# The recurrent mixer of a two-layer kernel: chunks inverted in pairs half a period apart, with the serial part one chunk behind

## The reference, cut to what matters

```python
def rwkv7_step(state, inp):
    r_t, w_t, k_t, v_t, kk_t, a_t = inp
    sa = jnp.einsum('bhvk,bhk->bhv', state, -kk_t)
    state = (state * w_t[:, :, None, :] + sa[..., None] * (kk_t * a_t)[:, :, None, :]
             + v_t[..., None] * k_t[:, :, None, :])
    y = jnp.einsum('bhvk,bhk->bhv', state, r_t)
    return state, y
...
    _, y = lax.scan(rwkv7_step, s0, (tm(rh), tm(wh), tm(kh), tm(vh), tm(kk), tm(ah)))
    mean = jnp.mean(y, axis=-1, keepdims=True)
    var = jnp.mean(jnp.square(y - mean), axis=-1, keepdims=True)
    y = (y - mean) * lax.rsqrt(var + GN_EPS)
...
    mix = jnp.concatenate([o_nsa, o_rwkv], axis=-1).astype(x.dtype)
    return x + mix @ w_out
```

## Time and profile before

| what | us |
|---|---|
| median of 3 runs | 2627.87 |
| lowest and highest of them | 2627.56 and 2632.1 |
| the profiled execution's own time | 2630.19 |
| its span, first to last instruction | 2628.2 |
| PE busy | 2567.8 |
| DVE busy | 1561.6 |
| ACT busy | 1108.6 |
| POOL busy | 425.6 |

### The profile page before, as it was taken

How to read it: one execution, slowest core, us unless ns; L and a number is a source line. 1 busy time by engine, 2 the same in 40 slices (tenths; PEclk the granted TensorE clock), 3 DMA queues, 4 the chain that set the end, 5 groups by cost and what they waited for, 6 DMA issues and landing times.

```text
span 2628.2 us, 46698 instructions
## 1 busy us (share of the span) xinstructions
PE 2567.8 (98%) x19224; PEld 2086.1 (79%) x19224; DVE 1561.6 (59%) x2521; ACT 1108.6 (42%) x2067; POOL 425.6 (16%) x381
## 2 busy tenths in 40 slices
PE   8999999999999999999999999999999999999998
PEld 6887777778778998899888777766776677788876
DVE  8765443436686665676546676355567646656754
ACT  3242233323355543556335554324445545344521
POOL 4421221100000000000000000111112100456644
PEclk9999999999999999999999999999999999999999
DMA  6753443134423454534534222631011253100032
GB/s 227 212 119 107 97 131 101 65 115 165 160 102 116 144 192 141 189 132 150 170 127 173 76 96 90 270 129 49 29 49 49 85 189 105 42 19 19 19 129 96
DMA packets 80754, 307.24 MB, mean 117 GB/s; under 512 B 7200, under 2 KB 8864, under 8 KB 62624
## 3 DMA queue, kind: packets, MB, share of 16 engines
q1 hardware_dynamic: 55984, 238.72, 25.9%
q0 software_dynamic: 12800, 33.56, 5.6%
q10 hardware_dynamic: 11760, 31.99, 3.2%
HBM read 268.32 MB, written 69.47 MB: 129 GB/s over the span
## 4 chain that ended last, share of the span: by engine, by line
PE 83%; DVE 9%; ACT 4%; issue 3%; DMA 1%; POOL 1%; DVEq 0%; ACTq 0%; SPq 0%; POOLq 0%
PE ps L425 46%; PE ps L3270 4%; PE ps L1258 4%; PE ps L1257 4%; PE ps L1259 4%; PE ps L2145 2%; PE ps L2191 2%; PE ps L2171 2%; PE ps L2072 2%; PE ps L609 2%; PE ps L635 1%; PE ps L2074 1%; PE ps L2073 1%; PE ps L624 1%; DVE parts L404 1%
## 5 line engine op out<-in xcount | busy, mean ns | idle before, releaser
L425 PE MATMUL ps<-parts,parts 128*128 128x512 f32 (+2 forms) x6456 | 1467.5, 387 | 15.9 <-DVE parts L804 8.8
L425 PEld LDWEIGHTS ps<-parts,parts 128*128 128x128 f32 x6456 | 1171.6, 188 | 299.7 <-issue 34.3
L404 DVE TENSOR_TENSOR parts<-ring,parts 128x1024 fp32r<-128x1024 f32 x180 | 220.8, 1238 | 174.7 <-ACT parts L381 166.3
L381 ACT CAST parts<-ring 128x1024 fp32r<-128x1024 f32 x183 | 188.7, 1044 | 116.9 <-DMA ring<-in_weights 62.1
L1257 PE MATMUL ps<-parts,parts 128*128 128x256 f32 x840 | 236.2, 281 | 1.3 <-ACT phase_data L1406 1.3
L1258 PE MATMUL ps<-parts,parts 128*128 128x256 f32 x840 | 236.1, 281 | 0.0
L1259 PE MATMUL ps<-parts,parts 128*128 128x256 f32 x840 | 236.0, 281 | 0.0
L404 POOL TENSOR_TENSOR parts<-ring,parts 128x1024 fp32r<-128x1024 f32 x62 | 153.2, 2472 | 423.1 <-DVE parts L381 423.0
L2552 POOL TENSOR_TENSOR phase_data<-phase_data,stream 128x512 f32<-128x512 f32 x12 | 17.2, 1436 | 1186.2 <-PE ps L2082 1186.2
L867 DVE TENSOR_TENSOR_SCAN stream<-stream 128x513 f32<-128x513 f32 (+3 forms) x96 | 95.2, 992 | 173.2 <-ACT stream L737 173.0
L1257 PEld LDWEIGHTS ps<-parts,parts 128*128 128x128 f32 x840 | 158.7, 189 | 2.4 <-ACT phase_data L1406 1.5
(11 more groups left out here) (391 smaller groups left out, 3761.6 us busy)
## 6 DMA issues: line engine op xcount, KB each, us to landing
ring<-in_weights SPq DMA_DIRECT2D x128, 1024.0 KB, 4.9
up_sums<-in_weights POOLq DMA_DIRECT2D x24, 1024.0 KB, 8.9
ring<-in_weights SPq DMA_DIRECT2D x32, 512.0 KB, 4.3
ring<-up_sums SPq DMA_DIRECT2D x30, 512.0 KB, 5.9
phase_data<-up_sums SPq DMA_DIRECT2D x60, 256.0 KB, 5.6
up_sums<-up_sums POOLq DMA_DIRECT2D x8, 1024.0 KB, 5.4
phase_data<-in_weights SPq DMA_DIRECT2D x30, 256.0 KB, 5.5
raw_keep<-phase_scratch SPq DMA_DIRECT2D x21, 256.0 KB, 2.4
```

The source lines that it names most:

```text
L381: cast(self.hi(p), self.whole(p)).then_inc(self.k.hi_ready, 1)
L404: g.tensor_tensor(self.lo(p), self.whole(p), self.hi(p).bitcast(F32), ALU.subtract).then_inc(self.k.lo_ready, 1)
L425: last = pe.matmul(out, a, b, start=i == 0 and a is ah and b is bh, stop=i == len(pairs) - 1 and a is al)
```

## The change: what it does

Every product of the inversion covers all four head pairs at once, so that there is one wait, one ACT copy and one DVE addition per product where there were two. The two banks of `inv_x` and the two of `inv_w` now belong to even and odd chunks. Iteration c (there are 18) holds levels 0 to 2 of chunk c, levels 3 to 5 of chunk d = c-1, and the serial part of chunk e = c-2. Level 5 multiplies only the 32x32 blocks that are not zero, from `mab` without a mask, so that POOL makes five masked copies and not six.

`raw`, `masked` and `both_heads` of chunk c+1 stay in iteration c, and the operands are made two chunks ahead on POOL, the exponentials three chunks ahead on ACT. There are more buffers for this: five for `ra`, three for `bk`, four for `mm`, three for `mab`. Two of the `ra` and one of the `mm` buffers lie in the ring slot of the third weight unit of the projection, which is therefore loaded only after the last `y_part`; another `mm` buffer lies in a place for a weight's high part.

The normalisation of the first four tiles stands in iterations 10 to 14 where it stood in 8 to 13. Half of projection tile 0 stands in iteration 16, the rest of it and two of eight parts of tile 1 in iteration 17.

The buffers and the loads:

```diff
@@ -2673,7 +2675,7 @@
         load_weights(k, sp, START["in3", 1] + 5)
         sp.wait_ge(gated, 8)
         sp.dma_start(io["mix_keep"], k.data(12544, 4096)).then_inc(k.spilled.sem, 16)
-        load_weights(k, sp, START["wout", 0] + RING)
+        load_weights(k, sp, START["wout", 0] + RING - 1)
         sp.wait_ge(raw_in, 48)
 
...
-    b.ra = [x.rearrange("p (c d) -> p c d", c=4) for x in (view_cp(k, 2560), low(0, 4 * P), low(512, 4 * P))]
+    lent = RING_AT + (START["wout", 0] + 2) % RING * SLOT
+    b.ra = [x.rearrange("p (c d) -> p c d", c=4) for x in (
+        view_cp(k, 2560), low(0, 4 * P), low(512, 4 * P), k.view(lent, 4 * P), k.view(lent + 512, 4 * P))]
...
-    mm, mab = low(3072, 4, 4 * P).rearrange("p (a b) (c d) -> p a b c d", a=2, c=4), four_of(low(5120, 2, 4 * CHUNK))
+    mab = four_of(low(5120, 2, 4 * CHUNK))
+    spare = HI_AT + (k.later_pieces.base + len(k.later_pieces.what) + 3) % 4 * (SLOT // 2)
+    mms = [four_of(x) for x in (low(3072, 2, 4 * P), low(4096, 2, 4 * P), k.view(lent + 1024, 2, 4 * P),
+                                k.data(spare, 2, 4 * P))]
+    mabs = (mab[:, 0], mab[:, 1], early(0, CHUNK))
...
-    x_bank, w_bank, G = (2, 4), (3, 7), (slice(0, 2), slice(2, 4))
+    XS, WS, TS, GS = LEVELS, LEVELS - 1, LEVELS - 1, LEVELS
+    x_bank, w_bank = (2, 4), (3, 7)
...
+    pieces.not_before[pieces.base + 4] = 2
...
         sp.wait_ge(y_mm, C)
+        load_weights(k, sp, START["wout", 0] + RING)
         sp.dma_start(gate[1], part("gate_keep", 1)).then_inc(gate_in[1], 16)
         x_again(1)
         load_weights(k, sp, START["wout", 0] + 4)
```

The body of `inv_x` and `inv_w`:

```diff
+            else:
+                pe.wait_ge(t_ready[i], TS * n + l)
+                if l < LEVELS - 1:
+                    pe.wait_ge(off_ready, MASKS * c + l + 1)
+                    last = product(c, x_out(c, l), off[:, i, l], tt[:, i])
                 else:
-                    pe.wait_ge(t_ready[i], (LEVELS - 1) * c + l)
-                    last = group_pairs(i, x_bank[i], 0, lambda m, e: off[rows(e), c % 2, l, m],
-                                       lambda m, e: tt[rows(e), 0, m])
-                last.then_inc(x_mm[i], 1)
+                    for m in range(4):
+                        for e in range(2):
+                            upper, lower = slice(64 * e, 64 * e + 32), slice(64 * e + 32, 64 * e + 64)
+                            last = pe.matmul(x_out(c, l)[lower, m, 0:32], mab(c)[upper, m, 32:64],
+                                             tt[upper, i, m, 0:32], start=True, stop=True)
+            last.then_inc(x_mm[i], 1)
...
+            i, n = c % 2, c // 2
+            pe.wait_ge(x_ready[i], TS * n + l)
+            pe.wait_ge(g_ready[i], GS * n + l)
+            if l < LEVELS - 1:
+                product(c, t_out(c), gg(c), xx[:, i])
+                last = product(c, w_out(c, l), xx[:, i], gg(c))
+            else:
+                for m in range(4):
+                    for e in range(2):
+                        upper, lower = slice(64 * e, 64 * e + 32), slice(64 * e + 32, 64 * e + 64)
+                        last = pe.matmul(w_out(c, l)[upper, m, 32:64], xx[lower, i, m, 0:32],
+                                         gg(c)[lower, m, 32:64], start=True, stop=True)
+            last.then_inc(w_mm[i], 1)
```

The order of PE:

```diff
-        for c in range(C + 1):
-            if c >= 1:
-                state_part(c - 1)
+        for c in range(C + 2):
+            d, e = c - 1, c - 2
+            if e >= 0:
+                state_part(e)
+            if 0 <= d < C:
+                turn(d)
             if c < C:
                 inv_x(c, 0)
-                turn(c)
-            else:
-                project(0, (0, 4))
-            if c >= 1:
-                solve(c - 1)
+            if 0 <= d < C:
+                inv_x(d, 3)
+            if c == C + 1:
+                project(0, (4, KT))
+            if e >= 0:
+                solve(e)
             if c < C:
                 inv_x(c, 1)
-                value_part(c)
+            if 0 <= d < C:
+                inv_w(d, 3)
+                value_part(d)
+            if c < C:
                 inv_w(c, 1)
+            if 0 <= d < C:
+                inv_x(d, 4)
+            if 10 <= c < 14:
+                mean(c - 10)
+            if 0 < c < C - 1:
+                raw(c + 1)
             if c == C:
-                project(0, (4, KT))
-                y_part(c - 1)
+                project(0, (0, 4))
+            if 0 <= d < C:
+                inv_w(d, 4)
             if c < C:
-                for l in range(2, LEVELS):
-                    inv_x(c, l)
-                    if l == 2 and c >= 1:
-                        y_part(c - 1)
-                        state_product(c - 1)
-                    if l == 3 and c + 1 < C:
-                        raw(c + 1)
-                    inv_w(c, l)
-                    if l == 3 and 8 <= c < 12:
-                        mean(c - 8)
-                    if l == 3 and 9 <= c < 13:
-                        bonus(c - 9)
-                    if l == 4 and 9 <= c < 13:
-                        variance(c - 9)
+                inv_x(c, 2)
+            if c == C + 1:
+                project(1, (0, 2))
+            if e >= 0:
+                y_part(e)
+            if 0 <= d < C:
+                inv_x(d, 5)
+            if c < C:
+                inv_w(c, 2)
+            if c == 0:
+                raw(1)
+            if 0 <= e < C - 1:
+                state_product(e)
+            if 0 <= d < C:
+                inv_w(d, 5)
+            if 10 <= c < 14:
+                variance(c - 10)
+                bonus(c - 10)
         for n in range(1, 16):
-            project(n)
+            project(n, (0 if n > 1 else 2, KT))
```

The order of ACT, cut:

```diff
+            d, e = c - 1, c - 2
+            if 0 <= d < C:
+                a.wait_ge(turn_mm, 2 * d + 1)
+                if d >= 2:
+                    a.wait_ge(s_mm, d - 1)
+                a.copy(bkt[:, d % 2], four(0, P)).then_inc(turn_read, 1)
+                copy_x(d, 3)
+                a.wait_ge(turn_mm, 2 * d + 2)
+                a.copy(uv[64:128, d % 2], four(1, P)[64:128]).then_inc(turn_read, 1)
             if c < C:
-                a.wait_ge(turn_mm, 2 * c + 1)
-                if c >= 2:
...
+                copy_x(c, 1)
+            if e >= 0:
+                a.wait_ge(u_mm, e + 1)
+                for h in range(2):
+                    a.copy(uv[0:64, e % 2, :, rows(h)], four(6)[rows(h)]).then_inc(u_ready, 1)
+            if 0 <= d < C:
+                copy_x(d, 4)
+            if c == C:
+                split_hi(0, 7)
+            if c + 3 < C:
+                exps(c + 3)
+            if 12 <= c < 15:
+                pieces.split_ahead(a, 0, most=c - 11)
             if c < C:
...
+                copy_x(c, 2)
+            if c == 0:
+                k.late_evict()
+            if 0 <= d < C:
+                copy_x(d, 5)
+            if 10 <= c < 14:
+                square(c - 10)
+            if c + 1 < C:
+                both_heads(c + 1)
+            if e >= 0:
+                a.wait_ge(y_mm, e + 1)
+                a.copy(A[:, :, at(e)], four(6)).then_inc(y_read, 1)
+            if 10 <= c < 14:
+                inverse_root(c - 10)
```

The order of DVE:

```diff
+        def open_inverse(c):
+
+            i, n = c % 2, c // 2
+            v.wait_ge(off_ready, MASKS * c + 1)
+            if c >= 3:
+                v.wait_ge(u_mm, c - 2)
+            v.tensor_tensor(gg(c), off[:, i, 0], bc(eye), ALU.add).then_inc(g_ready[i], 1)
+            v.wait_ge(x_mm[i], XS * n + 1)
+            v.tensor_tensor(tt[:, i], x_out(c, 0), bc(eye), ALU.add).then_inc(t_ready[i], 1)
...
+            if l < LEVELS - 1:
+                v.tensor_tensor(gg(c), gg(c), w_out(c, l), ALU.add).then_inc(g_ready[i], 1)
+            else:
+                for h in range(2):
+                    x = gg(c)[64 * h:64 * h + 32, :, 32:64]
+                    last = v.tensor_tensor(x, x, w_out(c, l)[64 * h:64 * h + 32, :, 32:64], ALU.add)
+                last.then_inc(g_ready[i], 1)
...
+                open_inverse(c)
+            if e >= 0:
+                combine(e)
+            if 0 <= d < C:
+                add_t(d, 3)
+                add_g(d, 3)
+                v.wait_ge(zv_mm, d + 1)
+                v.tensor_copy(zv[:, d % 2], four(0)).then_inc(zv_ready, 1)
+            if c < C:
+                add_t(c, 1)
+                add_g(c, 1)
...
+            if 0 < c < C - 1:
+                masked(c + 1, (0,))
+            if 0 <= d < C:
+                add_t(d, 4)
+            if 0 < c < C - 1:
+                masked(c + 1, (1,))
+            if 0 <= d < C:
+                add_g(d, 4)
+            if c < C:
+                add_t(c, 2)
+                add_g(c, 2)
+            if c == 0:
+                k.late_shift()
+                masked(1, (0, 1))
+            if 0 <= e < C - 1:
+                next_state(e)
+            if 0 <= d < C:
+                add_g(d, 5)
+            if 11 <= c < 15:
...
+        v.wait_ge(y_mm, C)
```

(21 more changed lines are left out.)

247 lines of the change are left out of this document (114 added, 133 removed).

## The result

| | before | after |
|---|---|---|
| median of 20 runs each, taken together (us) | 2629.28 | 2633.88 |
| ratio, with its 95% interval | | 1.0016 [1.0009, 1.0023] |
| profiled execution, its own time | 2630.19 | 2631.39 |
| its span | 2628.2 | 2629.4 |
| mean granted clock of TensorE | 0.997 | 0.993 |

One of the 20 runs before took 2809.3 us and is left out of the ratio; the other 19 lie between 2627.56 and 2632.1. The changed kernel is slower by 0.16%, with the whole interval above one. That is clear of the noise, and less than the 0.2% that I had taken as a change that can be told. I had forecast 2618.7. TensorE has 18.5 us less to do, and the time is not shorter. The span misses the forecast (2621.0 for the execution's own time, less 2.0, is 2619.0) by 10.4 us.

A forecast was written before the change was run, and what follows sets the result against it. TensorE bounds the recurrence, with at most 2.6 us of waits a period. Start, iterations 2 to 15 (211.6 us) and end gain 9.2 us: 2630.2 becomes 2621.0, and the median, 2.3 lower, 2618.7; range 2606 to 2628.

The forecast's parts named there:

- 14.7 + 14.5 (no `raw`, but POOL's other work): Sum for iterations 2 to 15: the two last iterations at 14.7 and 14.5 us, the second without `raw`.
- has until 2.27 of the next period: End of the plain period: the opening of `gg`, under POOL's copies, may last until 2.27 us into the next.
- My rival for "slower": Recurrence: POOL holds `next_state` and delays `gg`'s opening, `combine` and `solve`, 1.3 us in 13 periods, about 2636; chance 0.08.
- each of these ended within one step: Argument against the slower outcome: the two openings that had taken 1.27 us each ended within one POOL step.
- so no part of the sum is about the clock: Whole kernel: TensorE had its full clock throughout before the change, so the sum gave the clock no term.
- The start: Before iteration 2: POOL's masked copies and operands set the pace; iteration 2 counts from 2278.2, 6.5 us ahead.
- Plain periods: Recurrence, iterations without normalisation: 14.7 us each instead of 15.16, with `next_state` held by POOL's masked copies.
- Iterations 10 to 13: Iterations with normalisation: block sums of `mean`, `variance` and `bonus` stretch the four periods to 16.2 us each.
- Iterations 16 and 17 to the end of `y_part`: End of the recurrence: about 12.5 us, then 7.2 us, so that the last `y_part` ends at 2509.5.
- The queues behind it: After the last `y_part`: later weight load and DVE's splits put at 0 us, up to 4 us if late.

The follow-up runs named there:

- e1: Changed kernel, with POOL in iterations 14 and 15 waiting for DVE's opening of `gg` before a weight's low part: 2624.82 us, ratio 0.998 to the kernel before.
- e2: Changed kernel, with DVE's `take_bonus`, `finish` and `split_lo` moved off the place ahead of the opening of `gg`: 2622.21 us, ratio 0.997.
- e4: Changed kernel, with six extra, unused products on PE ahead of `solve` in iterations 14 and 15: 2626.55 us, ratio 0.9987.
- e3: Changed kernel, with both the edits of e1 and e2 (POOL's wait and DVE's new order): 2620.73 us, ratio 0.9963.
- e6: e3, with `raw` of chunk 1 and its masks moved ahead of chunk 0's level 2 `inv_w` and additions: 2618.5 us, ratio 0.9958.
- e5: e3, with SP loading each projection weight in the tail ahead of loads needed later: 2617.57 us, ratio 0.9954.
- e7: e3, with `state_product` ahead of level 2's `inv_w` on PE and `next_state` ahead of the two additions on DVE: 2614.23 us, ratio 0.9939.
- e8: e3, with the edits of e5, e6 and e7 together: 2605.46 us, ratio 0.9906.

## Why the prediction was wrong, by its own steps

**The step that failed** is a term of the sum for iterations 2 to 15: "14.7 + 14.5 (no `raw`, but POOL's other work)". It gives 29.2 for iterations 14 and 15; they took 37.09, 7.9 more. I had named "POOL's other work" and not asked where it falls, and had walked only a plain iteration. The words that `gg` "has until 2.27 of the next period" are true of that one. In iteration 14, DVE's own list puts four operations of 128x512 ahead of the opening (three in iteration 15), which then begins at 3.15, past that time, and just then meets POOL's low part of a weight, 2.33 us long. e1 removes the meeting and gets back 6.9 us; e2 removes the queue, the meeting goes by itself, and it gets back 9.4. My rival for "slower" had this mechanism, a hold of the opening that delays `combine` and `solve`. It priced it at 1.3 us in every period, with "each of these ended within one step" against it. That holds still, but the step can be L404's 2.33 us and not a mask's 0.71.

**The clock was in no term.** "so no part of the sum is about the clock" was a reading of the kernel before. It fell behind waits that the change makes. In iterations 14 and 15, e4 shows it to cost 2.8 us (1.26 + 1.50). In the tail it costs 1.4: from the block sum at 2554.25 to the next tile it is 2.77 us, and 1.39 in e3 from 2545.32, with the clock at 1.00. At the start it costs about 1.5 (e6). That makes some 5.7 us, an estimate from these rows.

**The start: 2278.2 forecast, 2280.21 measured, +2.0.** Most of this stands ahead of the stretch that I had reckoned, and in two rows, the first product of chunk 0 and POOL's masked copies of chunk 2:

```profile
2257.27 0.68 PE L3292 MATMUL ps<-phase_scratch,stream 64*64 64x64 f32 x16 [1.23 <-DVE stream L3682]
...
2280.09 3.66 POOL L3047 TENSOR_TENSOR stream<-normed,phase_scratch 128x256 f32<-128x256 f32 x5 [1.12 <-ACT normed L3041]
```

The sum took over 2255.51 for the first product, which now comes 1.76 us later: 0.7 from earlier phases, where the two kernels do the same, and the rest because PE waits for the opening of `gg` (0.85 us beside POOL) before it. From there to iteration 2 it is 22.94 us, and by my numbers 22.7. That is near, but by luck. I let POOL bind it, and POOL's chain took what I gave it (11.4 us for 11.5 from the first masks of chunk 1), only to stand idle for 1.12 us. What bound the stretch was `raw` of chunk 1, its masks, its copies, POOL's first mask and the opening of `gg` (0.93 us beside POOL), and the halved clock after PE's idle time. e6 shows it.

**Plain periods: 14.7 forecast, 14.26 measured, -3.6 in eight.** The mechanism was right and three sizes were off. `next_state`'s second operation took 0.75, where I had about 0.9. PE idled 0.39 and not 0.65 before `solve`. And the 16 records of a 32x32 product cost 0.37 us (L3347 at 2333.77 in the changed kernel, the next product at 2334.14), between my bounds of 0.25 and 0.49, of which I had taken the upper. The Trainium skill ("TensorE: Matmul & The Clock Gate", "Back-to-back issue gap") gives one issue floor for all products from 1 to 64 columns. These rows differ: 0.37 for 16 records of 32 columns, 0.47 for 16 of 64. Each matmul here also loads its weights, which are 32 columns wide instead of 64 as well, and no run separates the two.

**Iterations 10 to 13: 64.8 forecast, 65.42 measured, +0.6.** The last two took 16.5, since `finish` already pushed the opening of `gg` back; e2 makes them 16.25.

**Iterations 16 and 17 to the end of `y_part`: 19.7 forecast, 19.96 measured, +0.3.** Right: 12.35 for 12.5, and 7.61 for 7.2.

**The queues behind it: "so I put this at 0; if it is late by another block's time, up to 4 us".** It cost 3.2 us: from the end of `y_part` to the end it is 112.7 us, and by my numbers 109.5. I had asked when `variance` first needs DVE and found slack, but the wait came at the tail's fourth `variance`, 37 us after `y_part`. I had let the block land 7.5 us after its issue, as before, and it took 9.7, with another 1 MB in the same crowd. (That this 1 MB is the reason was not tested by itself.) So this cast came no earlier by however much PE did, and with it DVE's list: the next two casts stand at 2540.60 and 2550.93, before at 2540.31 and 2550.63. Some 1.4 of the 3.2 us is the clock. e5 loads the weights by need, and 2.7 us come.

These sum to 2.0 - 3.6 + 0.6 + 7.9 + 0.3 + 3.2 = 10.4 us, the miss of the span.

**What stays open.** The median of the changed kernel lies 2.5 us above its profiled execution. The clock goes with it: of its 20 executions the two with a mean clock of 0.994 took 2630.1 and 2631.2 us, the seven with 0.991 took 2634.8 on average, and the one with 0.990 took 2635.9 (the one traced: 0.993). So the clock seems to fall more often in some of them than in the one traced, but where, no trace shows. It fits that e4's median lies 7.3 us below the changed kernel's, and its profiled execution only 4.4. How long a wait must be for the clock to fall is open too: in the tail it fell after 2.22 us in the changed kernel and stayed at 1.00 after 2.79 us in e3. The cause of a lower clock at 2262 in e7 and e8 and not in e3 or e6 isn't settled either: up to chunk 0's level 1 these kernels have the same order.

## What to carry to other kernels

Walk the iterations that are unlike the plain one, operation by operation on every engine: a table of what stands ahead of the critical operation in each of them would have shown 2.7 us of delay in iterations 14 and 15. Put an engine's filler work behind the operation for which another engine waits, never ahead of it; and where two engines share a port, see which long instruction can stand beside a critical one. Before you count a gain, ask what behind it will not come earlier (a load, another engine's queue), and whether a new wait can make TensorE's clock fall.

## What the runs showed of the hardware

In the changed kernel, waits of PE of 3.49 and 3.96 us were each followed by the clock at 0.50 for some 3.4 us and by 1.3 to 1.5 us of loss, so that each cost the program 1.4 times its length. Added products in the wait, which did nothing useful, took that loss away (e4). Shorter waits did not all go the same way. After 2.22 us in the tail of the changed kernel the clock fell, and after 2.79 us in e3's it did not. In iteration 17 of e6 it fell after waits of 0.61 and 0.53 us that e3 has as well, at full clock.

When VectorE's opening with both inputs in SBUF began 0.21 us after POOL's L404 (2.33 us), it took 2.41 us and ended 0.3 after it. The Trainium skill ("SBUF — State Buffer", "Who interferes with whom") has a DVE instruction with two SBUF inputs contend with a GpSimd one that reads SBUF, the one that issues first keeping the port for the whole instruction. The trace agrees. POOL is lengthened too: five masked copies took 5.08 us in iteration 14, beside DVE's operations of 128x512, and 3.91 in a plain period of e3.
